# Order and buffers of a first mixer's lead-in, of two post-norm seams and of memory attention in a three-layer kernel

## The reference

```python
hn = rms_norm(x, norm_mix_pre)
proj = hn @ w_in                 # a_qk, a_v, gates, a_o, b_q, b_k, b_v, b_r, b_lr
qk = silu(dwconv3(a_qk) + b)     # 4 heads: q, k of 64, v of 128
h = mlstm(q, k, v, i, log_sigmoid(f)) both ways      # exponential gates, running max
o = gla(b_q, b_k, b_v, log_sigmoid(b_lr @ w2 + b) / 16) both ways
x = x + rms_norm(concat(y_a, y_b) @ w_out, norm_mix_post)
x = x + rms_norm(conv_ffn(rms_norm(x, norm_ffn_pre)), norm_ffn_post)
for l in range(2):
    h = rmsnorm(x, norm_mix[l])
    x = x + (pool_conv_mixer(h) if l == 0 else mla_attention(h))
    x = x + memory_cross_attention(rmsnorm(x), rmsnorm(mem))   # softmax(q k / 16) v, 4 heads of 256
    x = x + conv_ffn_2(rmsnorm(x))
return rmsnorm(x, final)
```

## Time and profile before

| | us |
|---|---|
| median of 3 runs (2134.78 to 2139.16) | 2138.57 |
| profiled execution | 2139.53 |
| its span, first to last instruction | 2137.7 |
| TensorE busy | 2050.5 (96%) |
| GpSimd busy | 1460.4 (68%) |
| VectorE busy | 1030.7 (48%) |
| ScalarE busy | 588.9 (28%) |

### The profile page before, as it was taken

The page is one execution under the profiler, slowest core; times in us unless marked ns, Lnnn a source line. Parts: engine busy times, 40 slices in busy tenths (PEclk is TensorE's granted clock), DMA queues, the critical chain, the costliest instruction groups (busy, mean ns, idle before and its releaser), DMA issues.

```text
span 2137.7 us, 25474 instructions
## 1 busy us (share of the span) xinstructions
PE 2050.5 (96%) x9406; PEld 1640.7 (77%) x9406; DVE 1030.7 (48%) x1572; ACT 588.9 (28%) x1109; POOL 1460.4 (68%) x723
## 2 busy tenths in 40 slices
PE   7999897999999799999999999999999999999997
PEld 5677676888888688786788888877768778888886
DVE  4347745423434889563643231373557364323134
...
DMA packets 55464, 187.75 MB, mean 88 GB/s; under 512 B 6080, under 2 KB 7872, under 8 KB 55264
## 3 DMA queue, kind: packets, MB, share of 16 engines
...
## 4 chain that ended last, share of the span: by engine, by line
PE 84%; DVE 10%; ACT 2%; issue 1%; POOL 1%; DMA 0%; SPq 0%; DVEq 0%; POOLq 0%; ACTq 0%
PE bank L584 25%; PE bank L586 25%; PE bank L585 25%; DVE bank L2232 3%; PE bank L946 2%; PE bank L1175 2%; PE bank L789 1%; PE bank L1189 1%; PE bank L1205 1%; DVE ssq L1843 1%; DVE qkL L2117 1%; DVE hnL L1850 1%; PE bank L741 1%; POOL wH L530 1%; DVE MIX L1935 1%
## 5 line engine op out<-in xcount | busy, mean ns | idle before, releaser
L530 POOL TENSOR_TENSOR wH<-raw,zero 128x1024 fp32r<-128x1024 f32 (+2 forms) x309 | 593.8, 1922 | 491.1 <-PE bank L586 483.4
L533 POOL TENSOR_TENSOR wL<-raw,wH 128x1024 fp32r<-128x1024 f32 (+2 forms) x309 | 738.8, 2391 | 24.2
L584 PE MATMUL bank<-hnH,wH 128*128 128x512 f32 (+1 forms) x1472 | 583.8, 397 | 36.6 <-DVE hnL L1850 32.6
L585 PE MATMUL bank<-hnL,wH 128*128 128x512 f32 (+1 forms) x1472 | 577.0, 392 | 0.0
L586 PE MATMUL bank<-hnH,wL 128*128 128x512 f32 (+1 forms) x1472 | 576.8, 392 | 0.0
L584 PEld LDWEIGHTS bank<-hnH,wH 128*128 128x128 f32 (+1 forms) x1472 | 276.5, 188 | 107.8 <-DVE hnL L1850 35.5
L586 PEld LDWEIGHTS bank<-hnH,wL 128*128 128x128 f32 (+1 forms) x1472 | 276.4, 188 | 61.5 <-issue 1.1
L585 PEld LDWEIGHTS bank<-hnL,wH 128*128 128x128 f32 (+1 forms) x1472 | 276.6, 188 | 61.2 <-issue 2.7
L584 PE MATMUL bank<-actH,wH 128*128 128x512 f32 x784 | 307.3, 392 | 0.0
L586 PE MATMUL bank<-actH,wL 128*128 128x512 f32 x784 | 305.1, 389 | 0.0
L585 PE MATMUL bank<-actL,wH 128*128 128x512 f32 x752 | 292.5, 389 | 0.0
...
## 6 DMA issues: line engine op xcount, KB each, us to landing
...
```

Of the source, the lines that this page charges most:

```text
L530: nc.gpsimd.tensor_tensor(wH[:, slot, 0:w], raw[:, slot, 0:w], nothing.broadcast_to([P, w]), ALU.add)\
L533: nc.gpsimd.tensor_tensor(wL[:, slot, 0:w], raw[:, slot, 0:w], wH[:, slot, 0:w].bitcast(F32), ALU.subtract).then_inc(split, 1)
L584: mm(out_, aH, bH, start=first, stop=False)
L585: mm(out_, aH, bL, start=False, stop=False)
```

## The change

1. Lead-in. lr and gates become one tile `lr_gates` of 48 columns (gates on partitions 32 to 47); POOL splits unit 0 by `split_lead` in four instructions that reorder the columns. SP loads x chunk 0 before unit 0, chunk 1 before unit 1, the other six before unit 2, and after it the constants and W2, which ScalarE's queue issued before. ScalarE loads its table ahead of the data and squares all chunks after their high parts. TensorE runs the key-query tiles 0 and 1 two and five chunks behind the gates; `first_sums` comes when tile 0 is done, `gate_columns` after tile 1, `cumulate` after tile 2 with 8 products for 20, `gate_rows` after tile 3. `guard_columns` and `spread_max(0)` (bank 0 for max0) move between the second and third unit of a_v, the evacuation of a_v behind the first decay on ScalarE.
2. Scores. Four DMAs copy qkA with its halves of the partitions exchanged into qkO; every second key block is computed from there, on the other half of the array.
3. Post-norms. Square, root, scaled value and new x live in PSUM banks; ScalarE copies the new x back to XT. `post_sums` replaces `row_sums`. The second post-norm's sum comes after memory key 0, and ScalarE makes the high halves of memory keys 0 to 3.
4. Memory attention. turn(h) goes ahead of values(h - 1) on TensorE, rows ahead of output_high on ScalarE, with tiles renumbered.

The diff, cut to its core:

```diff
-MEMORY += [POS["mem_k0", _i] for _i in range(4, 8)]
+MEMORY += [POS["mem_k0", _i] for _i in range(8)]
...
+TILES = [("lr_gates", 1), ("a_qk", (0,)), ("row_sum1", 1), ("col_sum1", 1), ("a_qk", (1,)), ("gate_cols", 1),
+         ("a_qk", (2,)), ("cum", 1), ("a_qk", (3,)), ("gate_rows", 2), ("a_v", 4), ("guard_cols", 1), ("max0", 1),
+         ("s0", 4)]
...
-    OWN_BANKS.update({f"max{_n}": [4], f"nd{_n}": [5, 6]})
+    OWN_BANKS.update({f"max{_n}": [4 if _n else 0], f"nd{_n}": [5, 6]})
...
+    return base + {"s": (0, 2, 6, 12), "t": (4, 8, 14, 18), "o": (10, 16, 20, 22)}[kind][h] + i
...
+POSTS = {"post0": ("w_out", (("norm_b", 2), ("w_out", 6))), "post1": ("ff0_d2", (("ff0_d2", 2), ("ff0_d2", 5)))}
...
+            def exchange():
+                for i in range(4):
+                    gone_wait(sp, TILE0["a_qk"] + i)
+                for pair in range(2):
+                    for half in range(2):
+                        sp.dma_start(qkO[64 - 64 * half:P - 64 * half, pair, :, :],
+                                     qkA[64 * half:64 * half + 64, pair::2, :]).then_inc(sig("exchanged"), 16)
...
+                if u0 == POS["b_qk", 0]:
+                    exchange()
...
+                    if u0 + i0 < 3:
+                        for c_ in ((0,), (1,), range(2, KD))[u0 + i0]:
+                            sp.dma_start(XT[:, c_, :], x_t[c_ * P:c_ * P + P, :]).then_inc(x_in[c_], 16)
...
+                    if u0 + i0 == 2:
+                        sp.dma_start(CT[:, :], consts).then_inc(tables_in, 16)
+                        sp.dma_start(W2[:, :, :], gla_w2).then_inc(tables_in, 16)
...
+            def split_lead():
+                pool.wait_ge(loaded[0], 16)
+                src = raw[:, 0, 0:8 * 48].rearrange("p (k c) -> p k c", k=KD)
+                hi, lo = (t[:, 0, 0:8 * 48].rearrange("p (k c) -> p k c", k=KD) for t in (wH, wL))
+                parts = ((slice(0, 32), slice(16, 48)), (slice(32, 48), slice(0, 16)))
+                for to, at_ in parts:
+                    ins = nc.gpsimd.tensor_tensor(hi[:, :, to], src[:, :, at_],
+                                                  nothing.unsqueeze(1).broadcast_to([P, KD, at_.stop - at_.start]), ALU.add)
+                ins.then_inc(hi_split, 1)
+                pool.wait_ge(hi_split, 1)
+                for to, at_ in parts:
+                    ins = nc.gpsimd.tensor_tensor(lo[:, :, to], src[:, :, at_], hi[:, :, to].bitcast(F32), ALU.subtract)
+                ins.then_inc(split, 1)
...
+            def lead_in(k):
...
+                cut = slice(k * 48, k * 48 + 48)
...
-                for b in range(NB):
-                    for heads, others, tri in ((slice(0, 4), range(0, b), upto), (slice(4, 8), range(b + 1, NB), since)):
-                        to = psum(n)[:, b * 8 + heads.start:b * 8 + heads.stop]
-                        for i, q in enumerate(others):
-                            mm(to, ones, logf[:, q, heads], start=(i == 0), stop=False)
-                        last = mm(to, tri, logf[:, b, heads], start=(len(others) == 0), stop=True)
+                sums = psum(n)[:, 0:8 * NB].rearrange("p (b h) -> p b h", b=NB)
+                for heads, tri in ((slice(0, 4), upto), (slice(4, 8), since)):
+                    mm(sums[:, :, heads], tri, logf[:, :, heads], start=True, stop=False)
+                    for apart in range(1, NB):
+                        later, earlier = slice(apart, NB), slice(0, NB - apart)
+                        to, src = (later, earlier) if heads.start == 0 else (earlier, later)
+                        last = mm(sums[:, to, heads], ones, logf[:, src, heads], start=False, stop=(apart == NB - 1))
...
-            project("a_qk", hnH, hnL, ready=lead_ready, lead=1, after={1: first_sums, 2: gate_columns})
-            project_natural("a_v", hnH, hnL, KD, NB, TILE0["a_v"], POS["a_v", 0], 4, after={1: cumulate, 2: gate_rows})
+            for k in range(KD):
+                wait_hn("mix_pre", k)
+                lead_in(k)
+                if k >= 2:
+                    key_query(0, k - 2)
+                if k >= 5:
+                    key_query(1, k - 5)
+            key_query(0, 6)
+            key_query(0, 7)
+            first_sums()
+            for k in range(3, KD):
+                key_query(1, k)
+            gate_columns()
+            for i, then in ((2, cumulate), (3, gate_rows)):
+                for k in range(KD):
+                    key_query(i, k)
+                then()
...
-                for j in range(NB):
+                other = slice(64 - 64 * (h % 2), P - 64 * (h % 2))
+                pe.wait_ge(sig("exchanged"), 16 * 4)
+                for j in range(0, NB, 2):
                     n = TILE0[f"s{h}"] + j
                     claim(n)
+                    claim(n + 1)
                     mm(psum(n)[:, :], qkA[rows, 2 + h // 2, j * P:j * P + P], qkA[rows, h // 2, :], start=True,
                        stop=True).then_inc(tile_done, 1)
+                    mm(psum(n + 1)[:, :], qkO[other, h // 2, 1, j * P + P:j * P + 2 * P], qkO[other, h // 2, 0, :],
+                       start=True, stop=True).then_inc(tile_done, 1)
...
+            def first_max():
+                pe.wait_ge(sig("rows_ready"), 1)
+                guard_columns()
+                spread_max(0)
+            project_natural("a_v", hnH, hnL, KD, NB, TILE0["a_v"], POS["a_v", 0], 4, after={1: first_max})
...
+            def post_sums(post):
+                n = TILE0[post]
+                gone_wait(pe, TILE0[POSTS[post][0]] + KD - 1)
+                claim(n)
+                mm(psum(n)[:, :], ones, ssq[:, :], start=True, stop=True).then_inc(tile_done, 1)
+            post_sums("post0")
...
-            for i in (0, 1):
-                memory_key(i)
-            row_sums(TILE0["post1"], "post1")
-            for i in (2, 3):
+            memory_key(0)
+            post_sums("post1")
+            for i in (1, 2, 3):
...
-                for h in range(4):
-                    if h < 3:
-                        scores(h + 1)
+                for h in range(3):
+                    scores(h + 1)
+                    turn(h)
                     if h > 0:
                         values(h - 1)
-                    turn(h)
+                turn(3)
+                values(2)
                 values(3)
...
-                norm_chunk("mix_pre", c_)
+                high(hnH[:, c_, :], XT[:, c_, :], v("mix_pre", c_))
...
+            for c_ in range(KD):
+                square(XT[:, c_, :])
...
+            conv_middle(0)
...
+            conv_act(0)
+            for i in range(1, 4):
+                conv_middle(i)
+                conv_act(i)
+            nc.scalar.preload_act_table_set("natural_log_exp_and_others")
...
+                if i == 0:
+                    first_values()
...
+            def post_chunk(n, m):
+                run(MIX[:, m, :], psum(n)[:, :], ACT.Copy).then_inc(sig("post_copied"), 1)
+                run(psum(n)[:, :], psum(n)[:, :], ACT.Square).then_inc(sig("post_sq"), 1)
...
+                for c_ in range(KD):
+                    act.wait_ge(sig("x_new"), first + c_ + 1)
+                    fresh = fresh_bank(post, c_)
+                    high(hnH[:, c_, :], fresh, v(next_norm, c_))
+                    run(XT[:, c_, :], fresh, ACT.Copy).then_inc(sig("x_copied_back"), 1)
+                    if c_ > 0:
+                        new_square(c_ - 1)
...
+                if 4 <= m < 7:
+                    memory_high(GATES + m - 4)
+                act.wait_ge(sig("post_sum"), m + 1)
+                post_chunk(TILE0["ff0_d2"] + m, m)
+            memory_high(GATES + 3)
+            post_norm("post1", "mix2_0")
...
+                    if h >= 1:
+                        rows(h - 1)
                     if h >= 2:
                         output_high(h - 2)
-                    if h >= 1:
-                        rows(h - 1)
+                rows(3)
...
+            def post_squares(name, m):
+                n = TILE0[name] + m
+                posts[0] += 1
+                dve.wait_ge(sig("post_sq"), posts[0])
+                if m == 0:
+                    free(nc.vector.tensor_copy(ssq[:, :], psum(n)[:, :]), n)
+                else:
+                    free(tt(ssq[:, :], psum(n)[:, :], ssq[:, :], ALU.add), n)
+                gone_wait(dve, n)
...
+                def new_low(c_):
+                    dve.wait_ge(sig("x_copied_back"), first + c_ + 1)
+                    low(hnL[:, c_, :], fresh_bank(post, c_), v(next_norm, c_), hnH[:, c_, :])
                 for c_ in range(KD):
-                    if c_ < KD - 1:
-                        scale(c_ + 1)
-                    posts[0] += 1
-                    dve.wait_ge(sig("post_scaled"), posts[0])
-                    stt(XT[:, c_, :], MIX[:, c_, :], v(gain, c_), XT[:, c_, :], ALU.mult, ALU.add)\
-                        .then_inc(sig("x_new"), 1)
+                    fresh = fresh_bank(post, c_)
```

(16 more changed lines are left out.)

171 lines of the change are left out of this document (86 added, 85 removed).

## The result

The changed kernel takes 2081.39 us in the median (2080.61 to 2083.03, 4 runs) beside 2138.86 for the kernel before on the same chip (2134.78 to 2141.67, 4 runs): a ratio of 0.9734, 95% interval 0.9717 to 0.9751, 57.5 us. The profiled execution took 2083.03, its span 2081.3. Forecast were 2085.0, with 2074 to 2100 as the range.

The account below looks back on a forecast made before the run. TensorE was taken as the bound, 84% of the chain that ended last. Savings 21.0 + 5.1 + 3.5 + 10 + 14 = 53.6 us from 2139.5 gave 2085.9, to the median 2085; range 2074 to 2100.

Parts of the forecast that it names:

- Lead-in: Everything up to the first weighted sum: gate tile, start, gate sums, head 0 scores and the stop, 21.0 us saved.
- Start: Lead-in: new load order lands unit 1 near 7.0, first 128-column matmul at 11.4; 3.3 us saved, bounds 1.1 to 3.4.
- Gate sums: Lead-in, cumulate: 16 instructions for 40 save 2.6 us, and the half clock behind them going saves 1.6.
- Stop: Lead-in, behind head 0's scores: max1's wait and half clock go, 6.3 us saved, less 0.7 charged for first_max waiting.
- Scores of the other heads: Scores of heads 1 to 3: neighbours on opposite array halves overlap, 1.7 us each, 5.1 saved, bounds 0 to 5.4.
- Seam after w_out: From w_out's last product to the feed-forward: VectorE's rows shorten with data in PSUM, 3.5 us saved, bounds 1.5 to 4.
- Seam before pc_in: Shorter VectorE rows, then POOL late next at the third tile; row_sum3 earlier by 8.5 to 10.8 us, 10 taken.
- POOL's relief of 2.3 us for each key: Seam before pc_in: ScalarE making the high halves of key units 0 to 3 takes about 2.3 us off POOL each.
- Memory attention: Two layers: turns ahead of values remove PX waits and slow values, 7.0 us each, 14.0 saved, bounds 6 to 14.4.
- A to C: Rivals: gate chain late, 2094 (0.15); memory attention gains half, 2092 (0.12); VectorE's seam rows stay long, 2095 (0.06).
- D: Rival: more goes, namely the half-clock spell at 138, POOL faster, half-clock stretches at the seams; 2077 us, chance 0.1.
- F: Rival: slower through TensorE falling to the half clock repeatedly; 268 extra slow matmuls turn the sign, 2145 with 300; chance 0.02.

Follow-up runs that it names:

- e2: The changed kernel with the old running gate sums, 40 instructions in place of 16, at their new place behind key tile 2: 2087.83 us.
- e1: The changed kernel with guard columns and max 0 again behind the scores of head 0, a_v's evacuation ahead of the guard: 2091.52 us.
- e3: The changed kernel without the exchange DMAs, all 16 score products from qkA, four one after another on the same 64 rows: 2096.7 us.
- e5: The kernel before the change with only the new order in memory attention: 2123.77 us, ratio 0.9924.
- e6: The changed kernel with root, scaled value and new x of both post-norm seams in SBUF again, squares still in PSUM: 2088.84 us.
- e7: The changed kernel with POOL making both halves of memory keys 0 to 3 again, without ScalarE's high halves: 2089.97 us.

## Why the prediction was right, step by step

1. Lead-in, 21.0 against 21.6. Right in sum and nearly in its parts. Start: 2.2 us for 3.3, since unit 1 was on hand at 8.12 and not 7.0; this term was too large. Gate sums: 4.3 for 4.2, by the rows of before; undone in the changed kernel they cost 5.9 (e2). Stop: 7.0 (e1) for 6.3, and first_max waited 0 where I charged 0.7, for a reason that I hadn't seen (e3). Scores of head 0: 1.7 (1.9 for 3.6). The 5.5 for one gate tile and the 0.7 for the chunks had no run of their own; with them the parts add up to 21.4. About 1 us of the agreement is luck: in the runs whose first products come 0.43 us apart until 16, as before the change, stage A is 76.7 to 77.2, a gain of 20.2 to 20.7.
2. Scores of the other heads, 5.1: 5.06 by e3. Stage B has 3.2 more, the half-clock spell of the earlier trace rows, which I had left at 0; it went, and the granted clock up to the last weighted sum is 1.00 now. What removed it is not shown: e3 has unpaired scores and no such spell either, and e5, the kernel before but for memory attention, still has it. Stage C gave 1.8 back, where the clock fell at 190; e2, whose trace has no spell there, has 153.2 in stage C, as before the change. So two terms that I put at nothing were 3.2 and -1.8; that they largely cancelled is luck. The Trainium skill, TensorEngine Tiling (Array Packing), Key Properties, says that a change of tiling mode drains TensorE; the trace agrees with a small cost: from the last product on 128 rows to the first score on 64 it is 0.32 us from start to start (66.87 to 67.19), where two on 128 rows are 0.23 apart.
3. Seam after w_out: 3.5 forecast, stage D 4.5, since the product with ones ran at the full clock (1.12 us), where I had worked with the half. The mechanism held for the chunks. The step that failed is the one after it, "so nothing more is lost": I had put the chunks at 2.1 to 2.2 us and looked only at TensorE's products. What I missed is that at this spacing the squares' additions behind the chunks come 2.9 us later, counted from the first product, that they have two SBUF inputs, and that they now meet POOL. Stage E took 1.9 back, in the long form 4.7, and then the whole seam is a loss of 0.9 (40.0 against 39.1). e6, with the chunks in SBUF, has them 1.9 apart and its additions done before POOL starts. The Trainium skill, SBUF - State Buffer, Who interferes with whom, has the rule that I used for the chunks (two SBUF inputs block against GpSimd, one doesn't); the trace agrees for the additions as well: 0.69 us alone and up to 2.8 beside POOL for two SBUF inputs, 0.70 beside it for one. I had weighed it for the instructions that the diff changes and not for those it leaves.
4. Seam before pc_in: 10 forecast, 10.4 measured, partly for a wrong reason. POOL was late next at the third tile and VectorE's rows were short (right). POOL's relief of 2.3 us for each key was 0.4 in all (wrong, e7). The size came out all the same: POOL's units behind the keys were split at 4.3 us each, as the sum had them, and without ScalarE's help the four keys take POOL 4.3 each too, while with it POOL stands waiting for ScalarE, 3.42 us for key 3 alone.
5. Memory attention: 14.0 against 15.2 to 15.4 (e5). Mis-sized by 1.3 us, just beyond the top of my bounds (14.4): in layer 0 it is 39.0 us from the first score to the first product behind attention before (981.86 to 1020.89) and 31.0 after (940.86 to 971.84), 8.05, of which I had priced only the two waits and the slow values. From start to start turn(2) took 4.64 us (1005.03 to 1009.67) for 0.88 now (964.50 to 965.38), values(2) 6.26 (to 1015.93) for 3.43, and turn(3) 1.83 (to 1017.76) for 0.88: 7.54, where I had 7.0. The other 0.5 are gaps too short to be marked, 0.3 of them ahead of values(1).

Of the rivals, A to C didn't happen, though A's mechanism is real (e3). D's kind of gain (the spell at 138, 3.2 us) came and was partly paid back in C (1.8). F's mechanism, the clock falling again in the 97 to 300 stretch and at the seams, is there, at a price of 1.8 us in stage C and 3.4 at the seam after w_out, far from the 53.6 that would turn the sign.
